# A hybrid decoder layer in split fp32: five matmuls per weight chunk in place of six, with the last columns summed on VectorE

## The reference, cut to what matters

```
h = rmsnorm(x, norm1);  z = h @ w_in            # 2048 x 3848
a, b, c = gMLP(z), sliding-window attention(z), mLSTM(z)
x = x + concat(a, b, c) @ w_out                 # 2048 x 2048
h = rmsnorm(x, norm2);  u = h @ w_up            # 2048 x 11264
g, v = split(causal depthwise conv of width 3 (u))
x = x + (silu(g) * v) @ w_down                  # 5632 x 2048
```

## Time and profile before

| | before |
|---|---|
| time, median of three runs | 2407.44 us (2404.39 to 2410.3) |
| profiled execution, span from first to last instruction | 2405.0 us |
| TensorE matmuls busy | 2286.1 us (95%), 18446 instructions |
| VectorE busy | 862.5 us (36%) |
| ScalarE busy | 730.5 us (30%) |
| GpSimd busy | 939.2 us (39%) |
| mean granted TensorE clock | 0.970 |

### The profile page before, as it was taken

How to read it: one execution, slowest core, us unless ns; L and a number is a source line. 1 busy time by engine, 2 the same in 40 slices (tenths; PEclk the granted TensorE clock), 3 DMA queues, 4 the chain that set the end, 5 groups by cost and what they waited for, 6 DMA issues and landing times.

```text
span 2405.0 us, 45377 instructions
## 1 busy us (share of the span) xinstructions
PE 2286.1 (95%) x18446; PEld 2213.2 (92%) x18446; DVE 862.5 (36%) x1465; ACT 730.5 (30%) x1259; POOL 939.2 (39%) x735
## 2 busy tenths in 40 slices
PE   6899999877799999999999999999999999999988
PEld 6899888664699999999999999999999999999987
DVE  5111224467622243333433333343333334333332
ACT  3222233135533333232323223232322323233232
POOL 3443232200244444444444444444444444444431
PEclk8899999787999999999999999999999999999999
DMA  6732222510333332323323232332323223232322
GB/s 153 182 97 74 73 71 81 62 51 23 111 89 99 93 90 88 89 90 92 104 88 90 89 88 90 91 105 88 90 89 88 90 90 106 87 92 89 88 71 97
DMA packets 323329, 217.37 MB, mean 90 GB/s; under 512 B 11414, under 2 KB 297215, under 8 KB 322367
## 3 DMA queue, kind: packets, MB, share of 16 engines
q1 hardware_dynamic: 309987, 207.64, 28.6%
q10 hardware_dynamic: 13182, 7.24, 2.7%
HBM read 201.36 MB, written 13.85 MB: 89 GB/s over the span
## 4 chain that ended last, share of the span: by engine, by line
PE 87%; issue 6%; DVE 4%; POOL 2%; ACTq 1%; ACT 0%; DMA 0%; DVEq 0%; SPq 0%; POOLq 0%
PE ps L414 59%; PE ps L708 21%; POOL wlo L1632 2%; DVE nvar L392 1%; PE ps L666 1%; PE ps L379 1%; PE ps L656 1%; DVE sx L1432 0%; PE ps L644 0%; PE ps L765 0%; PE ps L534 0%; PE ps L498 0%; PE ps L507 0%; PE ps L506 0%; ACTq L936 0%
## 5 line engine op out<-in xcount | busy, mean ns | idle before, releaser
L1632 POOL TENSOR_TENSOR wlo<-raw,whi 128x512 fp32r<-128x512 f32 x712 | 931.3, 1310 | 1426.6 <-ACT whi L808 1298.5
L808 ACT ACTIVATE whi<-raw 128x512 fp32r<-128x512 f32 x712 | 448.7, 632 | 1362.9 <-PE ps L414 983.1
L414 PE MATMUL ps<-h_hi,whi 128*128 128x260 f32 x2816 | 396.5, 283 | 14.3 <-issue 14.3
L414 PE MATMUL ps<-h_lo,whi 128*128 128x260 f32 x2816 | 394.3, 282 | 0.0
L414 PE MATMUL ps<-h_hi,wlo 128*128 128x260 f32 x2816 | 393.7, 282 | 0.0
L414 PEld LDWEIGHTS ps<-h_hi,whi 128*128 128x128 f32 x2816 | 360.0, 188 | 16.5 <-issue 16.1
L414 PEld LDWEIGHTS ps<-h_lo,whi 128*128 128x128 f32 x2816 | 361.4, 189 | 0.0
L414 PEld LDWEIGHTS ps<-h_hi,wlo 128*128 128x128 f32 x2816 | 361.4, 188 | 0.0
L414 PE MATMUL ps<-act_hi,whi 128*128 128x260 f32 x1504 | 219.6, 289 | 30.9 <-POOL wlo L1632 18.3
L414 PEld LDWEIGHTS ps<-act_hi,whi 128*128 128x128 f32 x1504 | 197.2, 192 | 39.4 <-issue 37.9
L1563 DVE TENSOR_TENSOR xT<-ps,xT 128x520 f32<-128x520 f32 x160 | 111.8, 699 | 287.9 <-PE ps L708 286.7
(11 more groups left out here) (296 smaller groups left out, 1457.5 us busy)
## 6 DMA issues: line engine op xcount, KB each, us to landing
raw<-in_w_up SPq DMA_DIRECT2D x88, 1024.0 KB, 5.4
raw<-in_w_down SPq DMA_DIRECT2D x44, 1024.0 KB, 4.9
raw<-in_w_in SPq DMA_DIRECT2D x30, 1024.0 KB, 5.1
raw<-in_w_out SPq DMA_DIRECT2D x16, 1024.0 KB, 5.7
x_spill<-xT SPq DMA_DIRECT2D x1, 4160.0 KB, 24.3
xT<-x_spill SPq DMA_DIRECT2D x1, 4160.0 KB, 12.4
xtok<-in_x_prompt SPq DMA_DIRECT2D x4, 1024.0 KB, 8.1
out_y_prompt<-ytok SPq DMA_DIRECT2D x4, 1024.0 KB
```

The lines of the kernel that those rows point to most:

```text
L414: mm = nc.tensor.matmul(ps[:, bank + h, 0:NH], w[:, k, c, :], x[:, 4 * c + k, h * NH:(h + 1) * NH], start=(k == 0 and kind == 0 and c == 0 ...
L808: nc.scalar.activation(whi[:, k, :, :], rawq(k, slot), ACT.Copy)\
L1632: nc.gpsimd.tensor_tensor(wlo[:, k, :, :], rawq(k, u), whi[:, k, :, :].bitcast(F32), ALU.subtract).then_inc(w_lo, 1)
```

## The change

Each chunk still puts the same 3 x 520 = 1560 columns through TensorE. They are cut differently, and the products with few tokens go to a second accumulator:

- In `tile_mm`, `whi` by `hi` for 348 tokens; `whi` by `hi` and by `lo` for the last 172 tokens in one matmul with two runs of 172 columns (read from `act_x[:, :, c, NF:N]`, written to two places of one bank); `whi` by `lo` for 348 tokens; `wlo` by `hi` for 260 tokens; and for the other 260. The last one, and the `lo` half of the two-run matmul, go to `rest`, which VectorE adds. The first chunk of each unit has six: its last 260 columns are two matmuls of 88 and 172.
- In `down_tile` the five have 380, 2 x 140, 380, 288 and 232 columns, with two extra accumulators, `d_low` (140 tokens) and `d_rest` (232 tokens).
- The `whi` matmuls of a tile come before its `wlo` matmuls, as before; the order inside `whi` alternates between `hi` and `lo` for each chunk.
- VectorE reads a unit with three operations, not one: 520 elements, `rest` times the scale in place in PSUM (260), and the sum (260), with a wait on its own semaphore before the last. For `w_out` it is two (520, 260). A down tile takes three (520, 232, 140), each waiting for the one before; only the last counts up `d_add`.
- `hi` and `lo` arrays become two planes of one tensor; sizes and waits between engines are otherwise the same.

```diff
+NT = 172
+NF = N - NT
+AT = 512 - NF
+DT = 140
+DF = N - DT
+DAT = 512 - DF
+DR = 512 - 2 * DT
...
+    flat = ps[:].rearrange("p b n -> p (b n)")
+    def body(b, lo=0, hi=N, rows=slice(0, P)):
+        return flat[rows, 512 * b + AT + lo:512 * b + AT + hi]
+    def rest(b, rows=slice(0, P)):
+        return flat[rows, 512 * b + AT + N:512 * b + AT + N + NH]
+    def d_body(b, lo=0, hi=N):
+        return flat[:, 512 * b + DAT + lo:512 * b + DAT + hi]
+    def d_low(b):
+        return ps[:, b + 1, DT:2 * DT]
+    def d_rest(b):
+        return ps[:, b + 1, 2 * DT:512]
...
-            for kind, (w, x) in enumerate(((w_h, x_h), (w_h, x_l), (w_l, x_h))):
-                for c in range(4):
-                    for h in range(2):
-                        mm = nc.tensor.matmul(ps[:, bank + h, 0:NH], w[:, k, c, :],
-                                              x[:, 4 * c + k, h * NH:(h + 1) * NH],
-                                              start=(k == 0 and kind == 0 and c == 0),
-                                              stop=(k == 3 and kind == 2 and c == 3))
+            start = 512 * (bank + 1)
+            ends = flat[:, start - (NH - NT):start + NH + NT].rearrange("p (a n) -> p a n", a=2)[:, :, NH - NT:NH]
+            for i in range(4):
+                c, f = 4 * i + k, k == 0 and i == 0
+                nc.tensor.matmul(body(bank, 0, NF), whi[:, k, i, :], x[:, 0, c, 0:NF], start=f, stop=False)
+                nc.tensor.matmul(ends, whi[:, k, i, :], x[:, :, c, NF:N], start=f, stop=False)
+                nc.tensor.matmul(body(bank, 0, NF), whi[:, k, i, :], x[:, 1, c, 0:NF], start=False, stop=False)
+            for i in range(4):
+                c, l = 4 * i + k, k == 3 and i == 3
+                nc.tensor.matmul(body(bank, 0, NH), wlo[:, k, i, :], x[:, 0, c, 0:NH], start=False, stop=l)
+                if k == 0 and i == 0:
+                    nc.tensor.matmul(rest(bank)[:, 0:NH - NT], wlo[:, k, i, :], x[:, 0, c, NH:NF], start=False, stop=False)
+                    mm = nc.tensor.matmul(rest(bank)[:, NH - NT:NH], wlo[:, k, i, :], x[:, 0, c, NF:N], start=False, stop=l)
+                else:
+                    mm = nc.tensor.matmul(rest(bank), wlo[:, k, i, :], x[:, 0, c, NH:N], start=False, stop=l)
             mm.then_inc(w_used, 1)
+        def down_tile(k, b):
+            ends = ps[:, b + 1, 0:2 * DT].rearrange("p (a n) -> p a n", a=2)
+            for c in range(GC):
+                f = c == 0
+                nc.tensor.matmul(d_body(b, 0, DF), whi[:, k, c, :], g_x[:, 0, c, 0:DF], start=f, stop=False)
+                nc.tensor.matmul(ends, whi[:, k, c, :], g_x[:, :, c, DF:N], start=f, stop=False)
+                nc.tensor.matmul(d_body(b, 0, DF), whi[:, k, c, :], g_x[:, 1, c, 0:DF], start=False, stop=False)
+            for c in range(GC):
+                l = c == GC - 1
+                nc.tensor.matmul(d_body(b, 0, N - DR), wlo[:, k, c, :], g_x[:, 0, c, 0:N - DR], start=False, stop=l)
+                mm = nc.tensor.matmul(d_rest(b), wlo[:, k, c, :], g_x[:, 0, c, N - DR:N], start=False, stop=l)
...
@@ reading a unit of w_in (the same for w_up, with rs2, into zg and za)
-            tt(halves(zT[:, u, :]), pair(2 * (u % 2)), halves(rs1[:]), mult).then_inc(z_free, 1)
+            b = 2 * (u % 2)
+            tt(zT[:, u, :], body(b), rs1[:], mult)
+            tt(rest(b), rest(b), rs1[:, NH:N], mult).then_inc(s("z_rest"), 1)
+            dve.wait_ge(s("z_rest"), u + 1)
+            tt(zT[:, u, NH:N], rest(b), zT[:, u, NH:N], add).then_inc(z_free, 1)
...
+        def add_down(e, n):
+            b = 4 + 2 * (e % 2)
+            tt(xT[:, e, :], d_body(b), xT[:, e, :], add).then_inc(s("d_body"), 1)
+            dve.wait_ge(s("d_body"), n)
+            tt(xT[:, e, N - DR:N], d_rest(b), xT[:, e, N - DR:N], add).then_inc(s("d_rest"), 1)
+            dve.wait_ge(s("d_rest"), n)
+            tt(xT[:, e, DF:N], d_low(b), xT[:, e, DF:N], add).then_inc(s("d_add"), 1)
```

More of the change, by code:

```diff
@@ L145, in hybrid_layer @@
     z2 = r_z.again()
-    h2_hi = z2.take("h2_hi", [P, KC, N], F32R)
-    h2_lo = z2.take("h2_lo", [P, KC, N], F32R)
+    h2_x = z2.take("h2_x", [P, 2, KC, N], F32R)
+    h2_hi, h2_lo = h2_x[:, 0], h2_x[:, 1]
     xT = r_x.take("xT", [P, KC, N])
@@ L288, in hybrid_layer @@
     fA = r_act.again()
-    g_hi = fA.take("g_hi", [P, GC, N], F32R)
-    g_lo = fA.take("g_lo", [P, GC, N], F32R)
+    g_x = fA.take("g_x", [P, 2, GC, N], F32R)
+    g_hi, g_lo = g_x[:, 0], g_x[:, 1]
     zg = fA.take("zg", [P, N + 2])
@@ L442, in _ @@
             pe.wait_ge(h_lo, 4 * (k + 1))
-            tile_mm(k, 4, whi, wlo)
+            tile_mm(k, 4, act_x)
         pe.wait_ge(s("rel_in"), 32)
@@ L696, in up_mm @@
                     before(k)
-                tile_mm(k, bank, whi, wlo, h2_hi, h2_lo)
+                tile_mm(k, bank, h2_x)
         def down_mm(q0, d0):
@@ L704, in down_mm @@
                 b = 4 + 2 * (k % 2)
[L705 to L710, removed]
+                down_tile(k, b)
                 yield k
@@ L1208, in _ @@
         r4, rf = slice(0, 4), slice(32, 36)
-        tt(halves(gf[rf, 0, :]), ps[rf, 4:6, 0:NH], halves(rs1[rf, :]), mult)
-        tt(halves(gi[:, 0, :]), ps[r4, 4:6, 0:NH], halves(rs1[r4, :]), mult).then_inc(s("c_gates_read"), 1)
-        dve.wait_ge(s("c_gates_read"), 1)
+        for g, rows in ((gf[rf, 0, :], rf), (gi[:, 0, :], r4)):
+            tt(g, body(4, rows=rows), rs1[rows, :], mult)
+            link(tt(rest(4, rows), rest(4, rows), rs1[rows, NH:N], mult))
+            tt(g[:, NH:N], rest(4, rows), g[:, NH:N], add).then_inc(s("c_gates_read"), 1)
+        dve.wait_ge(s("c_gates_read"), 2)
         link(ts(gf[rf, 0, :], gf[rf, 0, :], gbf[rf, :], None, add))
@@ L1487, in residual @@
             dve.wait_ge(w_used, i * 8 + (4 * u + 8))
-            x2 = xT[:, tile, :].rearrange("p a (h n) -> p (a h) n", h=2)
-            tt(x2, pair(2 * u), x2, add).then_inc(z_free, 1)
+            x2 = one(xT[:, tile, :])
+            tt(x2, body(2 * u), x2, add).then_inc(s("x_sum"), 1)
+            dve.wait_ge(s("x_sum"), n + 1)
+            tt(x2[:, NH:N], rest(2 * u), x2[:, NH:N], add).then_inc(z_free, 1)
             dve.wait_ge(z_free, n + (Z_N + 3))
@@ L1523, in read @@
                 dve.wait_ge(w_used, u0 * 4 + (4 * unit + 8))
-                tt(halves(z[:, 2:]), pair(bank), halves(rs2[:]), mult).then_inc(s(name), 1)
+                tt(z[:, 2:], body(bank), rs2[:], mult)
+                tt(rest(bank), rest(bank), rs2[:, NH:N], mult).then_inc(s(name + "_rest"), 1)
+                dve.wait_ge(s(name + "_rest"), n + 1)
+                tt(z[:, 2 + NH:], rest(bank), z[:, 2 + NH:], add).then_inc(s(name), 1)
                 dve.wait_ge(s(name), n + 1)
@@ L1588, in _ @@
             dve.wait_ge(w_used, 4 * (U_ALL - GC) + e + 5)
[L1589 to L1590 removed]
+            add_down(e, (NG - 1) * 16 + (e + 1))
             if e:
```

22 lines of the change are left out of this document (11 added, 11 removed).

## The result

| | before | after |
|---|---|---|
| time, median of five runs | 2407.44 us (2404.39 to 2410.3) | 2414.83 us (2411.14 to 2419.04) |
| profiled execution, span | 2405.0 us | 2413.1 us |
| TensorE matmuls busy | 2286.1 us, 18446 instructions | 2300.5 us, 15717 instructions |
| VectorE busy | 862.5 us | 1002.6 us |
| mean granted TensorE clock | 0.970 | 0.968 |

The changed kernel takes 1.0036 of the time before, 95% interval 1.0022 to 1.0049: 0.4% slower with 2729 matmuls fewer. Timed again beside later experiments it was 2410.79 us (2409.04 to 2417.4) against 2408.39 us, ratio 1.0019 (1.0003 to 1.0035). So the loss is small, some 2 to 7 us, and both intervals lie above 1.

What follows compares the result with a forecast made beforehand. TensorE, busy 95% of the span, was taken as the bound, at 120 ns per matmul. Matmuls -16.8, stalls +14 and end +0.8 gave -2.0 us: 2403 us span, 2405 us median; range 2340 to 2440.

Steps and rivals of the forecast that it cites:

- I take 11.7 ns per matmul: TensorE's fp32r stream: each matmul costs 11.7 ns plus columns / 2.4; fewer matmuls in units and down tiles save 16.8 us.
- The argument from the half clock: At 1.2 GHz 260 columns take 217.5 ns with no rest, which a fixed rate per column at both clocks would not do.
- cost per column: Rival, 18%: the matmul stream costs 0.4615 ns per column and nothing per matmul; 2437 us.
- The same 120 ns for units and down tiles: Matmuls of units and down tiles both priced at 120 ns before the change, a chunk of six at 0.720 us.
- First chunk "92 more": Each unit's first chunk, with 88- and 172-column matmuls at a 112 ns floor, costs 812 ns, 92 more than before.
- Down chunk "8 less": A five-matmul chunk of the down tiles takes 712 ns, 8 less than before; 704 chunks give 5.9 us.
- Stalls of "1.4 us per group": TensorE waits for VectorE's down sums before down tiles 2 and 3, 0.5 and 0.9 us; 14 us in 10 groups.
- VectorE falls further behind: Rival, 2%: VectorE's waits on itself are 0.2 us, not 0.035, stalling two or three more tiles per group; 2420 us.
- End, 0.8 us: At the kernel's end the last `xT` sum stands alone on the path and adds 0.8 us.
- The two-run matmul pays twice: Rival, 14%: each run of the two-run matmul costs its own 11.7 ns, six handovers per chunk as before; 2437 us.
- The larger fixed part: Rival, 24%: the 120 ns are mostly handover or a floor under which columns are free; 2333 us, or about 2363.

Runs made afterwards that it cites:

- experiment 2: Changed kernel with each unit's first chunk cut as 348, 172, 260, 260, 260, 260, without the 88-column matmul: 2408.58 us, ratio 1.0009 to the kernel before.
- experiment 7: Kernel before with other matmul widths: 512 columns; 128, 192 and 240; 348 and 380; one column read 260 times: 2356.05, 2346.36, 3104.21 and 2379.4 us.
- Experiment 1: Kernel before with only the last 260 columns of each unit's first chunk split into 88 and 172: 2424.55 us, ratio 1.007.
- experiment 5: Changed kernel with one more 520-element VectorE operation before the value-half read, once per loop group: 2429.12 us, ratio 1.0098 to the kernel before.
- experiment 6: Changed kernel run once more, unedited: 2410.79 us, ratio 1.0019 to the kernel before.
- experiment 3: Changed kernel with the old down tiles (six matmuls of 260 columns, one VectorE sum): 2407.86 us, ratio 1.0007 to the kernel before.

## Why the prediction was wrong

The forecast was -2 us, by two large terms that nearly cancel. Both were mis-sized, in opposite directions: 24 us of error in the matmuls and 12.5 in the stalls. The error of the sum, 4 to 9 us, is small only because they partly cancel.

- **"I take 11.7 ns per matmul": the step that failed.** In streams of one width the measured fixed part is 5.1 ns; of the 11.3 that 119.6 ns leave, the other 6.2 scale with the columns (0.4405 ns each where 1 / 2.4 is 0.4167). An ordinary chunk of the changed kernel saves 4.8 ns on average and not 11.7, and only 0.8 with the first chunk of experiment 2. The argument from the half clock did not hold: at 1.2 GHz both parts vanish at all three widths seen there (experiment 7), so that row could not tell them apart. By the prediction's own 2.7 us per ns this step alone is worth 18 us. The *cost per column* rival was right in the main: it is most of the overhead, and part of it is the reading of moving columns (experiment 7, one column).
- **The same 120 ns for units and down tiles.** The earlier trace rows gives 119.4 for a unit's matmul, and so 11.1 and not 11.7 to be saved. By that a unit would give 73 ns and not 84, which is 1.5 us in all: a small slip beside the step above.
- **First chunk "92 more".** With three ordinary chunks at 712 the first tile leaves 2967 - 3 x 712 = 831 ns for it, 19 more than priced; that split is an estimate, since the later tiles differ among themselves. The floor of 112 ns for the two short matmuls was right as a level in a stream of short ones; 88 columns cost more than that because the two matmuls behind it are held as well. With 15 x 4.8 = 72 ns gained and 119 lost, a unit loses 47 ns where 84 were to be gained: +6.3 us for 134, not -11.3. Experiment 1 shows the price of the split alone (+113 ns); experiment 2 shows that avoiding it does not bring the gain.
- **Down chunk "8 less".** It is 1.8 more (721.8 ns): +1.2 us for 176 tiles, not -5.9 (8 x 704 is in fact 5.6). Of it, 5 ns are the smaller fixed part's, and 4 are open.
- **Stalls of "1.4 us per group"** were 0.15, 1.5 us and not 14. The durations, the read's growth and the order of who waits for whom were right (experiment 5). Missed was that VectorE's old time held three collisions with GpSimd, 0.80 for the copy, 0.44 for `ca` and 0.38 for the product, which go away as the added work shifts them. The added 0.82 us of the read were cancelled by the copy's 0.80: down(0,0) starts 3.86 us after the first down matmul, exactly as before. *VectorE falls further behind* did not happen.
- **End, 0.8 us: right.** The sum of tile 15 ends and the transposes start, as in the earlier trace rows:

```profile
2396.60 0.70 DVE L1571 TENSOR_TENSOR xT<-ps,xT 128x520 f32<-128x520 f32 x1 [1.68 <-PE ps L468]
...
2397.76 0.30 DVE L1575 TENSOR_TENSOR xT<-ps,xT 128x140 f32<-128x140 f32 x1
...
2398.12 0.66 PE L820 MATMUL ps<-ident,xT 128*128 128x128 f32 x4 [0.69 <-DVE xT L1575]
```

- **The two-run matmul pays twice: no.** 344 columns in two runs take 157.4 ns, 348 in one 159. The sentence of the Trainium skill, "PSUM — Partial Sum Buffer", section Specifications, that was cited is not borne out for two runs of 172 columns.
- **The larger fixed part: no.** 348 columns take 159 ns and not its 147. Nor is the present 120 ns a load floor: with half the weights it stays at 119.5.
- **Not foreseen.** At each turn of the loop TensorE stands still for `issue`. From 1060 to 2320 us that is 1.55 us a turn before and 1.18 after:

```profile
PE ps L414 <- issue: 12.4, 8, 1.7
```

```profile
PE ps L444 <- issue: 10.6, 9, 1.5
```

The first is of the kernel before. What shortens it was not tried; it gives back 3.3 us in nine turns. It also differs between executions: in that of experiment 6 it is 1.24 us a turn.

The sum of what was measured: 6.3 + 1.2 + 1.5 + 0.8 - 3.3 = +6.5 us, against +7.4 in the first timing and +2.4 in the second. That it meets the first so closely is luck: 6.6 us of the first profile's loss came from ahead of the up units, where the sum has 2.2 (46 units at 47 ns). Behind them the sum has 4.3 and the profiles show 3 to 3.6. VectorE's busy time was forecast as 1100 us and came to 1003; the shorter copies and products are part of that difference.

Open: the 4 ns per chunk in mixed widths, why the three later tiles of a unit take 2828, 2852 and 2868 ns behind one first tile and 2859, 2869 and 2867 behind a shorter one (experiment 2), what a unit without any short matmul would take (none was run), why the old down tiles are 7 ns shorter beside the new layout than in the kernel before (experiment 3), and what sets the granted clock between 500 and 640 us.

## What to carry to other kernels

Fewer, wider matmuls pay only what a matmul costs beyond its columns, and a trace with one width can't tell that. Before an edit that rests on it, run the stream once with another width and take the line, and then time the mix itself: here the line promised 5 ns per merged matmul, and mixed chunks without a short matmul gave 1 to 3. One narrow matmul in a stream of wide ones can cost more than many merged ones save: here 113 ns for the one of 88 columns, against 72 for fifteen. And when VectorE's chain has little slack, look at which of its instructions end together with a GpSimd one: their length is not their own, and moving them may give or take more than the work that is added.

## What the runs showed of the hardware that was not expected

- fp32r at full granted clock, in streams of one width with 128 x 128 weights: 5.1 ns per matmul and 0.4405 ns per column through 260, 348, 380 and 512 columns, and 112 ns for 128, 192 and 240; with one moving column repeated, 112.5 ns for 260. At half the clock, medians of 218, 291 and 427 ns for 260, 348 and 512.
- Chunks of 1560 columns in five matmuls of mixed widths take 716 to 717 ns, 4 more than that line gives, whichever of the two cuts without an 88- or 232-column matmul is taken.
- Splitting one 260-column matmul into 88 and 172 columns makes a unit 113 ns longer, though the next one starts 43 ns after the 88-column one.
- VectorE's copy of 128 x 10 elements takes 0.17, 0.26 or 1.06 us, and its 8-element operation 0.22, 0.66 or 1.32, by how much of a GpSimd subtraction is left when it starts; sums that read PSUM are not held up, and GpSimd's 1.29 us become 1.53 or 1.82 in the other order.
